# Writing out TensorE's first seven expert items in a two-layer decoder kernel

## The chip, the core and the metric

The kernel runs on one core of one Trainium2 chip. A core has five engines with an instruction stream each: TensorE (PE in the profile), VectorE (DVE), ScalarE (ACT), GpSimd (POOL) and SyncE (SP), and 16 DMA engines that move data between HBM and the on-chip memory (SBUF). TensorE's results go to PSUM, which has eight banks. The engines order their work by semaphores alone. The metric is the device time of one execution in microseconds, the median of several.

## The reference

The input is 256 tokens of width 1024 in float32, the weights are float32 too. Layer 0 is a gated linear recurrence with a dense SwiGLU, layer 1 is a sparse attention followed by a mixture of experts, in which each token goes to two of eight experts. The last part, which the change touches, computes this:

```python
def moe_swiglu(xn, w_router, w_gu, w_down):
    logits = (xn @ w_router).astype(jnp.float32)
    top_v, top_i = lax.top_k(logits, TOP_K)
    top_w = jax.nn.softmax(top_v, axis=-1)
    ...
    for e in range(N_EXPERTS):
        out = out + gates[..., e:e + 1] * swiglu(xn, w_gu[e], w_down[e]).astype(jnp.float32)
```

`w_gu[e]` is 1024 x 7168 (gate and up side by side) and `w_down[e]` is 3584 x 1024: 44.04 MB for one expert, 352 MB for all eight.

## The kernel before, in words

**Stages.** Everything up to the router takes the first 580 us. Then come the *items*. An item is one expert with a tile of up to 96 of the tokens that chose it. Each expert has at least one item; an expert with more than 96 tokens gets another. So there are at least E = 8 items, and the number, which depends on the data, is computed by VectorE and put into SBUF (`route[0:1, ITEMS:ITEMS + 1]`, semaphore `counted`). In the execution shown there are eight.

**One item on TensorE** (lines 2023 to 2033) is 48 *chunks* of weights. A chunk is 128 x 1792 floats, 896 KB by the profile (917,504 bytes). Their order is the table `ITEM`: gate and up of the first half of the hidden columns, gate of the second half, half of the first down part, up of the second half, and the rest. For a gate or up chunk `input_chunk` multiplies the tokens `XT` in three groups of 32 by the chunk, which gives 12 matmuls of 448 columns, each on 32 columns of the array; for a down chunk `down_row` does 12 matmuls of 256 columns for each row of the chunk. Each float32 matmul stands as two in the trace, so that one item has 1440 of them.

**Buffers for the weights.** There are DEEP = 12 slots (six in `ring`, six in `more`). SyncE issues the DMA for chunk m + 12 when TensorE has done with chunk m: `load_item`, lines 672 to 683, waits for `chunk_used` or for a full bank. Chunk m is waited for in `chunk_arrived`, line 543.

**Loops.** All five engines walk over the items in a loop of their own with the item's number in a register. SyncE's covers items 1 to 7 (line 699), with further ones under a condition; ScalarE's is at line 1202 (silu of the gates, copies of the result), VectorE's at line 1579 (product, transposes, and the token tile of the next item with `x_ready`), GpSimd's at line 891 (it loads the rows of a coming item and stores the rows of the one that is done). TensorE's is at line 1986: it waits for `counted`, reads the number of items from SBUF into a register (line 1985), and every wait in the body has a value computed from the loop register, as in

```python
    eng.wait_ge(ready, 16 * (before + m // DEEP + 1) + i * (16 * PER_ITEM // DEEP))
```

Of the kernel before, what the change touches and what calls it, by code (L numbers as in the profile page):

```python
# [58 lines left out]
E, ED = 8, 3584  # L59
# [3 lines left out]
ITEMS = 16  # L63
# [208 lines left out]
def trunk(nc, ins, out):  # L272
# [5 lines left out]
    with ctx:  # L278
# [3 lines left out]
        def sem(name):  # L282
            return ctx.enter_context(nc.semaphore(name))
# [36 lines left out]
        def area(at, *shape, parts=P):  # L320
            n = int(np.prod(shape))
            assert at + n <= AR, (at, n)
            v = arena[0:parts, at:at + n]
            if len(shape) == 1:
                return v
            letters = "abcd"[:len(shape)]
            return v.rearrange(f"p ({' '.join(letters)}) -> p {' '.join(letters)}",
                               **{x: s for x, s in zip(letters[1:], shape[1:])})
# [87 lines left out]
        route = area(11090, 2 * ITEMS).bitcast(I32)  # L416
# [37 lines left out]
        counted, routed = sem("counted"), sem("routed")  # L454
# [80 lines left out]
        def chunk_slot(m):  # L535

            s = m % DEEP
            if s < RING:
                return ring[:, s, 0:WIDE], slot_ready[s], RAW_BASE[s]
            s -= RING  # L540
            return more[:, FIRST_FREE[s // 2] + PAIRS * (s % 2), 0:WIDE], more_ready[s], 0

        def chunk_arrived(eng, m, i):

            v, ready, before = chunk_slot(m)
            eng.wait_ge(ready, 16 * (before + m // DEEP + 1) + i * (16 * PER_ITEM // DEEP))
            return v
# [20 lines left out]
        def bank_count(name, i):  # L568
            b, k = JTURN[name]
            return b, JBASE[b] + k + i * JPER[b]  # L570
# [1042 lines left out]
        def _(pe):  # L1613
            ident, ones, halves = K("ident"), K("ones"), K("halves")

            def mm(o, w, x, start, stop, **kw):
                return pe.matmul(o, w, x, start=start, stop=stop, **kw)  # L1617
# [351 lines left out]
            def gather(n):  # L1969

                b = 6 + n
                for m in range(4):
                    d = 4 * n + m
                    for tt in range(TT):
                        last = mm(ps[:, b, TILE * m:TILE * m + TILE], acc[:, tt, :].rearrange("p (f c) -> p c f", c=KC)[:, d, :], sel[:, tt, :], tt == 0, tt == TT - 1)
                last.then_inc(bank_full[b], 1)
# [4 lines left out]
            for n in range(2):  # L1981
                free_bank(pe, ("gather", n))
                gather(n)
            pe.wait_ge(counted, 1)
            n_items = pe.value_load(route[0:1, ITEMS:ITEMS + 1], min_val=E, max_val=ITEMS - 1)
            with pe.Fori(0, n_items) as i:
                def free(name):
                    b, k = bank_count(name, i)
                    pe.wait_ge(bank_free[b], k)
                    return b  # L1990

                def input_chunk(m, kind, j, c):

                    w = chunk_arrived(pe, m, i)
                    for a in range(GROUPS):
                        b = free((kind, j, a)) if c == 0 else JTURN[(kind, j, a)][0]
                        for n in range(4):
                            last = mm(ps[32 * n:32 * n + 32, b, 0:QUARTER], XT[:, a, c, :], w[:, QUARTER * n:QUARTER * n + QUARTER],
                                      c == 0, c == KC - 1)
                        if c == KC - 1:  # L2000
                            last.then_inc(bank_full[b], 1)
                    if m not in FILLS:
                        last.then_inc(chunk_used, 1)

                def down_row(j, r):

                    first, final = j == 0 and r == 0, j == TILES - 1 and r == ROWS_DN - 1
                    for a in range(GROUPS):
                        b = JTURN[("y", a // 2)][0]
                        if first and a % 2 == 0:  # L2010
                            free(("y", a // 2))
                        at = PIECE * (a % 2)
                        for n in range(4):
                            q, piece = divmod(4 * r + n, PIECES)
                            w = chunk_slot(CHUNK_AT[("dn", j, q)])[0]
                            last = mm(ps[32 * n:32 * n + 32, b, at:at + PIECE], HT[j][:, a, r, :], w[:, PIECE * piece:PIECE * piece + PIECE],
                                      first and a % 2 == 0, final, skip_group_check=True)
                        if final and a:
                            last.then_inc(bank_full[b], 1)
                    if not final and any((4 * r + n) % PIECES == PIECES - 1 for n in range(4)):  # L2020
                        last.then_inc(chunk_used, 1)

                pe.wait_ge(x_ready, i + 1)
                for m, (kind, j, q) in enumerate(ITEM):
                    if kind != "dn":
                        input_chunk(m, kind, j, q)
                        continue
                    if q == 0:
                        pe.wait_ge(hidden_turned, i * TILES + j + 1)
                    chunk_arrived(pe, m, i)  # L2030
                    for r in range(ROWS_DN):
                        if (4 * r + 3) // PIECES == q:
                            down_row(j, r)

# [1 line left out]
_OUT = (1, T, D)  # L2037
# [20 lines left out]
```

## Time and profile before

| | us |
|---|---|
| median of 3 runs | 1516.02 (1512.35 to 1521.06) |
| the profiled execution | 1516.77 |
| its span in the trace | 1515.1 |
| TensorE busy in the span | 1428.1 (94%) |
| VectorE, ScalarE, GpSimd busy | 435.6, 317.1, 149.7 |
| share of TensorE in the chain that ended last | 91%, "issue" 3% |

The span runs from the first to the last instruction that the profiler recorded. "The chain that ended last" is followed back from the last instruction: at each step to what released it, or to the instruction before it on its engine. "Issue" in that chain is time in which the engine waited for nothing that the profile shows. The granted clock is that of TensorE, as a share of 2.4 GHz: 1.0 is the upper level and 0.5 the lower, 1.2 GHz. The DMA share is the mean busy share of the 16 DMA engines; GB/s is what they moved.

### The profile page before, as it was taken

Reading aid. Unit: us, or ns where it says so; the run is one execution under the profiler, and the core shown is the slowest. Engines: PE = TensorE matmul, PEld = TensorE weight load, DVE = VectorE, ACT = ScalarE, POOL = GpSimd, SP = SyncE. Lnnn points to the kernel's source line nnn. Section 1 sums busy time; section 2 is a strip of 40 time slices with the busy share of each in tenths; the row PEclk is TensorE's granted clock in tenths of the full one; section 3 lists DMA queues with packets and bytes.
Section 4 is the critical chain, followed back from the end, with each engine's and each line's share of the span. In section 5 each row is a group of like instructions: output and inputs, shape, how many; then the busy total and the mean of one; then the engine's idle time right before and its main releaser. Section 6 shows DMA issues by size and latency. Waiting matters only on the chain.

```text
span 1515.1 us, 35581 instructions
## 1 busy us (share of the span) xinstructions
PE 1428.1 (94%) x15792; PEld 866.4 (57%) x15792; DVE 435.6 (29%) x645; ACT 317.1 (21%) x507; POOL 149.7 (10%) x219
## 2 busy tenths in 40 slices
PE   8999899999998899998998998998998998998995
PEld 7998799999896584343343343343343343344343
DVE  6864555555557821110110110110110110110111
ACT  5833443443446831000000000000000000000000
POOL 0600010000122715001001001001001001001001
PEclk9999999999998997999999999999999999999998
DMA  9760255555998045999999999999999999999992
GB/s 298 236 200 24 85 168 188 174 178 188 134 294 288 1 164 223 399 418 386 418 410 362 408 407 352 406 406 358 419 408 344 419 410 345 411 410 359 414 418 83
DMA packets 132794, 455.03 MB, mean 300 GB/s; under 512 B 12451, under 2 KB 74108, under 8 KB 132642
## 3 DMA queue, kind: packets, MB, share of 16 engines
q1 hardware_dynamic: 126386, 435.15, 75.2%
q0 software_dynamic: 6080, 17.37, 5.0%
q8 instruction: 136, 2.23, 0.6%
q10 hardware_dynamic: 176, 0.14, 0.0%
q14 instruction: 16, 0.13, 0.0%
HBM read 436.51 MB, written 14.55 MB: 298 GB/s over the span
## 4 chain that ended last, share of the span: by engine, by line
PE 91%; issue 3%; DVE 2%; ACT 2%; DMA 1%; POOL 0%; ACTq 0%; POOLq 0%; DVEq 0%
PE ps L1617 91%; DVE arena L1462 1%; DVE arena L1459 1%; DMA arena<-item_rows,arena 0%; ACT arena L1131 0%; DMA arena<-in_norm_mix_g 0%; ACT x_hi L930 0%; PE ps L1628 0%; PE ps L1865 0%; ACT x_hi L960 0%; DVE arena L1463 0%; ACT between L1152 0%; POOL arena L792 0%; PE ps L1635 0%; ACT arena L1028 0%
## 5 line engine op out<-in xcount | busy, mean ns | idle before, releaser
L1617 PE MATMUL ps<-more,arena 128*32 128x448 f32 x3456 | 328.9, 539 | 0.0
L1617 PE MATMUL ps<-ring,arena 128*32 128x448 f32 x2688 | 275.0, 569 | 31.7 <-issue 30.3
L1586 DVE TENSOR_TENSOR arena<-arena,ps 128x448 f32<-128x448 f32 x48 | 29.8, 621 | 811.0 <-PE ps L1617 807.4
L1617 PEld LDWEIGHTS ps<-more,arena 128*32 128x32 f32 x3456 | 105.8, 110 | 218.9 <-issue 218.9
L1617 PEld LDWEIGHTS ps<-ring,arena 128*32 128x32 f32 x2688 | 85.5, 115 | 213.0 <-issue 211.5
L1617 PE MATMUL ps<-ring,between 128*32 128x256 f32 x3360 | 189.2, 379 | 0.0
L511 DVE TENSOR_TENSOR w_lo<-ring,w_hi 128x2048 fp32r<-128x2048 f32 x67 | 153.3, 2291 | 78.1 <-ACT w_hi L505 78.1
L1617 PEld LDWEIGHTS ps<-ring,between 128*32 128x32 f32 x3360 | 105.5, 110 | 85.8 <-issue 8.1
L505 ACT ACTIVATE w_hi<-ring 128x2048 fp32r<-128x2048 f32 x67 | 127.7, 1911 | 102.8 <-PE ps L1617 96.7
L1617 PE MATMUL ps<-x_hi,w_hi 128*128 128x256 f32 x800 | 113.0, 293 | 9.7 <-ACT x_hi L930 4.4
L1209 ACT ACTIVATE arena<-ps 128x448 f32<-128x448 f32 x48 | 26.1, 544 | 456.5 <-PE ps L1617 456.5
L1617 PE MATMUL ps<-more,between 128*32 128x256 f32 x2016 | 115.3, 379 | 0.0
L1617 PEld LDWEIGHTS ps<-x_hi,w_hi 128*128 128x128 f32 x800 | 103.7, 197 | 15.8 <-issue 10.3
L1617 PE MATMUL ps<-x_lo,w_hi 128*128 128x256 f32 x800 | 105.9, 286 | 0.0
L1617 PE MATMUL ps<-x_hi,w_lo 128*128 128x256 f32 x800 | 104.2, 283 | 0.0
L1617 PEld LDWEIGHTS ps<-x_lo,w_hi 128*128 128x128 f32 x800 | 101.6, 196 | 0.0
L1617 PEld LDWEIGHTS ps<-x_hi,w_lo 128*128 128x128 f32 x800 | 99.6, 192 | 0.1
L881 POOL DMA_DIRECT2D item_rows<-arena x32 | 17.6, 550 | 802.4 <-ACT arena L1216 799.5
L1216 ACT ACTIVATE arena<-ps 128x512 f32<-128x512 f32 (+1 forms) x16 | 7.0, 487 | 427.2 <-PE ps L1617 427.2
L1617 PEld LDWEIGHTS ps<-more,between 128*32 128x32 f32 x2016 | 64.2, 110 | 44.8
L1617 PE MATMUL ps<-hid,w_hi 128*128 128x256 f32 x352 | 63.8, 283 | 0.0
L1617 PE MATMUL ps<-arena 128*128 128x128 f32 (+4 forms) x304 | 51.3, 370 | 7.8 <-DVE arena L1508 2.2
(260 smaller groups left out, 1072.6 us busy)
## 6 DMA issues: line engine op xcount, KB each, us to landing
more<-in_moe_w_gu SPq DMA_DIRECT2D x144, 896.0 KB, 7.8
ring<-in_moe_w_gu SPq DMA_DIRECT2D x112, 896.0 KB, 7.5
ring<-in_moe_w_down SPq DMA_DIRECT2D x80, 896.0 KB, 7.8
more<-in_moe_w_down SPq DMA_DIRECT2D x48, 896.0 KB, 7.8
ring<-in_ffn_w_gu SPq DMA_DIRECT2D x22, 1024.0 KB, 5.1
ring<-in_a_w_in SPq DMA_DIRECT2D x16, 1024.0 KB, 10.6
ring<-in_ffn_w_down SPq DMA_DIRECT2D x11, 1024.0 KB, 5.0
ring<-in_w_kv SPq DMA_DIRECT2D x6, 1024.0 KB, 5.1
```

The costliest lines, as they stand in the source:

```text
L505: eng.activation(w_hi[:, m, :], src, ACT.Copy).then_inc(hi_ready[m], 1)
L511: eng.tensor_tensor(w_lo[:, m, :], ring[:, RAW[name][0], :], w_hi[:, m, :].bitcast(F32), ALU.subtract).then_inc(lo_ready[m], 1)
L881: pool.dma_start(rows_i[:, :, PIECE * n:PIECE * n + PIECE].rearrange("o (a t) d -> t (o a) d", t=32), yt[32 * n:32 * n + 32, :, :]).then_i ...
L1209: act.activation(SU[:, a, :], ps[:, b, 0:QUARTER], ACT.Silu).then_inc(bank_free[b], 1)
L1216: act.activation(yt[:, groups, :], ps[:, b, 0:PIECE * (2 - n)].rearrange("p (a d) -> p a d", d=PIECE), ACT.Copy).then_inc(bank_free[b], 1)
L1459: dve.tensor_tensor(lb, ps[:, k, 0:2 * w].rearrange("p (b t) -> p b t", b=2), BD[:, h:h + 1, T - w:T].to_broadcast([P, 2, w]), ALU.add).th ...
L1462: link(dve.reduce_max(RM[:, s, :], lb, AX.X))
L1586: dve.tensor_tensor(SU[:, a, :], SU[:, a, :], ps[:, b, 0:QUARTER], ALU.mult).then_inc(bank_free[b], 1)
L1617: return pe.matmul(o, w, x, start=start, stop=stop, **kw)
```

## The change

TensorE's loop body becomes a function `item_products(i)`. It is called seven times with a number, i = 0 to 6, and then once inside a loop over the items from 7 on. So the seven calls stand in TensorE's program one behind the other with constant waits, and reading the number of items comes after them. No other engine's program changes, nor does any buffer, transfer or order of matmuls.

```diff
@@ -1981,9 +1981,7 @@
             for n in range(2):
                 free_bank(pe, ("gather", n))
                 gather(n)
-            pe.wait_ge(counted, 1)
-            n_items = pe.value_load(route[0:1, ITEMS:ITEMS + 1], min_val=E, max_val=ITEMS - 1)
-            with pe.Fori(0, n_items) as i:
+            def item_products(i):
                 def free(name):
                     b, k = bank_count(name, i)
                     pe.wait_ge(bank_free[b], k)
@@ -2032,6 +2030,13 @@
                         if (4 * r + 3) // PIECES == q:
                             down_row(j, r)
 
+            for i in range(E - 1):
+                item_products(i)
+            pe.wait_ge(counted, 1)
+            n_items = pe.value_load(route[0:1, ITEMS:ITEMS + 1], min_val=E, max_val=ITEMS - 1)
+            with pe.Fori(E - 1, n_items) as i:
+                item_products(i)
+
```

The end of an item and the start of the next in TensorE's program before: the last chunk's matmuls stand ahead of the branch (line 1986), which goes back to the start of the body. (`more`, `ring` and `between` are weight slots and hidden values in SBUF.)

```order
1408 L1617 MATMUL ps<-more,between 32x256 [waits more_ready5]
1409 L1617 MATMUL ps<-more,between 32x256 x23
1410 L1986 REGISTER_ALU
1411 L1986 COMPARE_AND_BRANCH
1412 L278 UNCONDITIONAL_BRANCH
```

The start of the body, to which the branch returns:

```order
1264 L1985 TENSOR_LOAD arena [waits counted]
1265 L1985 ISA x2
1266 L1986 UNCONDITIONAL_BRANCH
1267 L1986 ISA
1268 L546 ISA [waits x_ready]
1269 L1989 ISA [waits slot_ready0]
1270 L1617 MATMUL ps<-ring,arena 32x448 [waits bank_free0]
1271 L1617 MATMUL ps<-ring,arena 32x448 x3
```

In the changed program the end of item 0 and the start of item 1 stand in a row; such a place comes six times:

```order
1381 L1617 MATMUL ps<-more,between 32x256 [waits more_ready5]
1382 L1617 MATMUL ps<-more,between 32x256 x23
1383 L1617 MATMUL ps<-ring,arena 32x448 [waits bank_free0,slot_ready0,x_ready]
1384 L1617 MATMUL ps<-ring,arena 32x448 x3
1385 L1617 MATMUL ps<-ring,arena 32x448 [waits bank_free1]
1386 L1617 MATMUL ps<-ring,arena 32x448 x3
```

No register instruction and no branch stands between them any more. Between item 6 and item 7 the reading of the number of items and the entry into the loop stand now:

```order
2095 L1617 MATMUL ps<-more,between 32x256 [waits more_ready5]
2096 L1617 MATMUL ps<-more,between 32x256 x23
2097 L2036 TENSOR_LOAD arena [waits counted]
2098 L2036 ISA x2
2099 L2037 UNCONDITIONAL_BRANCH
2100 L2037 ISA
2101 L546 ISA [waits x_ready]
2102 L1987 ISA [waits slot_ready0]
2103 L1617 MATMUL ps<-ring,arena 32x448 [waits bank_free0]
```

These instructions have moved from ahead of item 0 to ahead of item 7. The loop's own branch still stands at the end of the body, behind item 7.

## Rows read from the trace of the kernel before

**Rows 1.** Waits of TensorE from 560 us on: total us, times, longest.
```profile
PE ps L1617 <- issue: 30.3, 7, 5.0
```

**Rows 2.** The chain that ended last, in order: start us, duration us, what.
```profile
580.88 110.89 PE ps L1617 x1440
691.77 5.05 issue
696.82 110.95 PE ps L1617 x1440
...
812.00 111.38 PE ps L1617 x1440
...
927.90 111.46 PE ps L1617 x1440
...
1043.40 110.04 PE ps L1617 x1440
...
1157.45 111.03 PE ps L1617 x1440
...
1273.04 111.26 PE ps L1617 x1440
...
1388.19 109.64 PE ps L1617 x1432
...
1510.80 1.28 DVE arena L1604
```

**Rows 3.** Line 1986, TensorE's loop: count, duration ns min/median/max, first and last start.
```profile
L1986 PEldq COMPARE_BRANCH  x8: 79/5144/5999, 690.4 to 1496.9; - x8
```

**Rows 4.** The same line from 690 to 692 us alone.
```profile
L1986 PEldq COMPARE_BRANCH  x1: 5999/5999/5999, 690.4 to 690.4; - x1
```

**Rows 5.** Stretches behind item 0: length, busy us by engine, granted clock, DMA share, GB/s.
```profile
691.80:694.00 2.20, 0.00 (x0) 0.00 (x0) 0.00 (x0) 0.56 (x2) 0.78 (x2) 1.00 1.04 425
...
696.80:701.00 4.20, 4.18 (x24) 1.20 (x28) 0.00 (x0) 0.00 (x0) 0.00 (x0) 0.50 1.02 413
701.00:702.00 1.00, 1.00 (x12) 0.32 (x8) 0.00 (x0) 0.00 (x0) 0.00 (x0) 0.73 0.89 374
```

**Rows 6.** Line 1985, reading the number of items: duration ns, start us.
```profile
L1985 PEldq TENSOR_LOAD <-arena x1: 487/487/487, 575.0 to 575.0; - x1
L1985 PEldq SEQ_ASSERT  x1: 24/24/24, 575.8 to 575.8; - x1
```

**Rows 7.** Line 1597, VectorE's last step for the next item's tokens: first and last start.
```profile
L1597 DVE TENSOR_TENSOR arena<-arena,x_gain x8: 957/958/960, 669.5 to 1475.9; 128x768 f32<-128x768 f32 x8
```

**Rows 8.** Waits of SyncE from 581 to 1498 us: total us, times, longest.
```profile
SPq L683 <- PE ps L1617: 478.0, 244, 18.9
SPq L680 <- PE ps L1617: 219.0, 128, 2.2
```

**Rows 9.** DMA from 697 to 808 us (item 1): packets and MB, all and by queue.
```profile
DMA packets 7279, 44.86 MB, mean 404 GB/s; under 512 B 893, under 2 KB 893, under 8 KB 7265
...
q0 software_dynamic: 379, 0.77, 2.3%
q8 instruction: 12, 0.20, 0.7%
```

**Rows 10.** DMA from 722 to 760 us.
```profile
DMA packets 2491, 15.91 MB, mean 419 GB/s; under 512 B 275, under 2 KB 275, under 8 KB 2488
```

**Rows 11.** Three stretches of 5 us while rows are stored and loaded (columns of rows 5).
```profile
700.00:705.00 5.00, 5.00 (x52) 1.50 (x44) 0.00 (x0) 0.00 (x0) 1.20 (x3) 0.85 0.95 356
705.00:710.00 5.00, 5.00 (x56) 1.59 (x52) 0.00 (x0) 0.00 (x0) 1.22 (x3) 1.00 1.03 328
710.00:715.00 5.00, 5.00 (x60) 1.64 (x56) 0.00 (x0) 0.00 (x0) 0.00 (x0) 1.00 1.01 330
```

**Rows 12.** Issue to landing of line 683's chunks, 655 to 692 us.
```profile
DMA to landing us min/median/max: 12.9/14.6/15.5
```

**Rows 13.** The same, 1005 to 1039 us.
```profile
DMA to landing us min/median/max: 6.4/7.2/8.0
```

## The prediction

> **What bounds the kernel now.** I read the page first: TensorE is busy for 94% of the span and holds 91% of the chain that ended last, so the question is what stands between its matmuls. TensorE's waits from 560 us on come next [rows 1]: the only large entry is "issue", 30.3 us in seven pieces, the longest 5.0 us. It is a wait for nothing that another engine or a DMA does. The chain in order of time [rows 2] shows where the seven are: one behind each of the first seven items. An item is a solid block of 1440 matmuls, and between the end of item 0 at 691.77 and the start of item 1 at 696.82 there is nothing. From start to start an item takes 115.9 us (696.82 - 580.88).
>
> What the pause is, the rows of TensorE's loop line tell [rows 3]: eight compare-and-branch instructions, with a median of 5144 ns, a longest of 5999 and a shortest of 79. Eight items end with eight branches; seven go back and the last falls through. The first starts at 690.42 and lasts 6.0 us, until 696.42 [rows 4], and the array starts at 696.82. The array ran out at 691.77, so the sequencer had been about 1.35 us ahead of it. The branch is thus the pause: 6.0 - 1.35 + 0.4 = 5.05.
>
> The pause has a second price [rows 5]. The granted clock is 1.00 until 694.00 (2.4 GHz), and it is 0.50 (1.2 GHz) for the 4.2 us after the restart and 0.73 in the next. So some 4.7 us of matmuls run at half rate, which costs 2.4 us more.
>
> The second resource near its limit is the stream of weights. The DMA share is about 1.0 through the items, and an item needs 44.86 MB [rows 9]. But SyncE waits 697 us in total (478.0 + 219.0) for TensorE to free a slot [rows 8], and TensorE never waits for a chunk: today the stream follows TensorE.
>
> **The change, part by part.**
>
> *Seven branches leave the path.* Six boundaries become plain sequence, and at the seventh, between items 6 and 7, the loop is entered rather than repeated. With eight items the loop runs once, and its one branch falls through, as the 79 ns one does. So all seven pauses go, not six: 30.3 us [rows 1].
>
> *Seven cold restarts leave too.* Items 1 to 7 take 110.95, 111.38, 111.46, 110.04, 111.03, 111.26 and 109.64 us [rows 2], together 775.76. Item 1 without its 2.4 us is 108.6; item 0, which also starts cold, stays as it is. I take 108.5 for a warm item, so the seven give back 775.76 - 7 x 108.5 = 16.3 us. Together with the pauses: 46.6 us.
>
> *The entry into the loop before item 7.* Reading the number starts at 575.0 in the old program and its check comes at 575.8 [rows 6]; with the register instructions behind it I count 1.0 us of the sequencer. That fits into its lead of 1.35 us [rows 4], so I take 0. The load did not wait for the array there: at 575.0 the gather products still ran. If the cover is missing, the price is 1 us; the upper end, if entering the loop breaks the stream like a branch does, is one whole pause with its cold restart, 6.7 us ((30.3 + 16.3) / 7). Both `counted` and the number were there 900 us earlier.
>
> *Constants in place of register arithmetic.* The matmuls' pace inside an item is the array's, and it is the same at item ends as in the middle; I take 0, and bound it by 0.3 us an item on either side, half the spread that is left between the items.
>
> *What is late next at a boundary: tokens and banks.* The next item's tokens are ready when VectorE's last step ends, 669.5 + 1.0 us for item 1 [rows 7], 21 us ahead of the end of item 0. Neither `x_ready` nor the gate banks, which ScalarE empties long before, can take the place of the branch: 0 us.
>
> *What is late next: the weights.* This is the term that takes something back. TensorE would use an item's 48 chunks in 108.5 us, 2.26 us each. What the DMA engines can do when there is always work waiting is seen right behind item 0, where the backlog is longest: 419 GB/s from 722 to 760 us [rows 10]. An item is 44.04 MB of weights, 0.79 MB of rows in and out, and 0.20 MB of instructions (the two last as in [rows 9], where the first rows are cut off), 45.0 MB: 107.5 us at 419 GB/s. While the rows move, in small packets, the rate is lower: 356, 328 and 330 GB/s in three stretches of 5 us [rows 11], which loses 5 x (0.15 + 0.22 + 0.21) = 2.9 us. So the stream needs 110.4 us an item, 1.9 more than TensorE.
>
> Against this stands a reserve. A slot comes round every 12 x 2.26 = 27.1 us, and TensorE waits only when issue to landing takes longer than that. At the end of item 0 it is 14.6 us [rows 12], a reserve of 12.5 us. Today every pause lets the stream catch up, and the time to landing is down to 7.2 us by item 3 [rows 13]. Without pauses it grows by 1.9 us an item instead, over seven items by 13.3 us: the reserve is just used up in item 7, and TensorE waits some 0.8 us. The bounds: if an item needs only 109.7 us, no wait at all; if its mean rate is the 404 GB/s that item 1 had over all of its length, 45.0 MB take 111.4 us, the deficit is 2.9 x 7 = 20.5 us and the wait 8 us. Since the reserve is so nearly gone, I take 2 us, nearer to the lower end.
>
> The Trainium skill gives a lower rate for the stream: in "DMA: Bandwidth & Descriptors", section "Bandwidth", some 358 GB/s from HBM for one core where both cores of a domain stream. By that an item would need 123 us and nothing could be gained. The trace disagrees for a core alone, with the 419 GB/s of the row above.
>
> *The sum.* The profiled execution took 1516.8 us, of which 1515.1 are its span. 1516.8 - 30.3 - 16.3 + 2 = 1472.2 us. What lies behind the last item (1497.8 to 1512.1, [rows 2]) moves as it is. The execution is 0.8 us above the median of the runs shown, which spread by 8.7 us: I leave 1472.
>
> **The rivals.**
>
> *The weight stream becomes the bound early.* Every item then takes what the stream needs. For it: a DMA share of 1.0, and a rate of 404 GB/s over item 1. Against it: that stretch holds the rows' slow time already, and 419 was held for 38 us. With 111.4 us an item it is 1472.2 - 2 + 8 = 1478; at 113 us the deficit is 4.5 x 7 = 31.5, less the reserve 12.5, so 19 us of waits: 1489. I name 1483 for the case.
>
> *One pause stays at the entry into the loop:* 1472 + 6.7 = 1479. For it: a branch of the same line number stands there. Against it: in the old program the same four instructions passed without a pause between 575.0 and 580.9.
>
> *Nothing is gained.* This would be so if the stream already needed all of the 115.9 us, the pauses being hidden in it: 1516. Against it speaks that TensorE never waits for a chunk, and that the time to landing falls from 14.6 to 7.2 us.
>
> *Slower: the long program cannot be fetched in time.* An item is 12 packets of the instruction queue, 16 KB each (0.20 MB by 12, [rows 9]), and seven items in a row are 84. Should a part of each fetch be exposed, the array waits at 84 places instead of seven. A branch shows a fetch to last 5 us. The change turns into a loss from 46.6 / 84 = 0.55 us exposed in each; with 1 us it is 1472 + 84 = 1556. Against it: the loop fetches 12 packets in each round now as well, so its body is read in sequence from memory too, and TensorE's blocks show no pause inside.
>
> The Trainium skill says of this in "Runtime: NRT & Kernel Launch", section "Instruction fetch mechanics", that instructions are read ahead in sequence in blocks of 16 KB and that a taken branch whose target is outside the window must wait for a fetch. The trace agrees, with 5.1 us for the branch and packets of that size. In "Advanced Engine Details and Errata", section "Control Flow Timing", a compare-and-branch costs about 108 ns; by that the seven would be worth 0.8 us and the kernel would stay at 1516. Only the branch that falls through, 79 ns, is near it.
>
> **How the numbers follow.** The forecast's case (1467 to 1477) has a chance of 0.68, the early bound by the stream 0.18, a pause left at the entry 0.06, nothing gained 0.04, slower 0.04. What a measurement of this kernel can tell from no change is about 0.5%, 7.6 us. The first three are all faster by over 0.5%: 0.92. No change 0.04, slower 0.04. The range runs from 1466, which allows no wait for chunks and an execution at the lower side of the spread, to 1485, into the middle of the second case; some 0.15 is left outside.
>
> **What would show it.** In the profile after, no "issue" pause of 4 to 5 us between the items, and at most one branch on TensorE's sequencer longer than 0.1 us (none, by the forecast). The items start 108.5 us apart from item 1 on, with a granted clock of 1.0 throughout. The time from issue to landing grows from item to item, from about 15 us to 25 or more in the last, and waits of TensorE for `ring` or `more` come only in items 6 and 7. I am wrong if TensorE waits for chunks from item 2 or 3 on (the stream's rate was mis-sized), if pauses appear inside the items, or if a pause stands before item 7.

## The result, and the profile after

| | us |
|---|---|
| before, median | 1516.24 (1512.35 to 1521.06, 4 runs) |
| changed kernel, median | 1478.36 (1474.24 to 1483.14, 4 runs) |
| ratio | 0.975, 95% interval 0.9709 to 0.9791 |
| profiled execution, span | 1479.12, 1477.5 (before 1516.77, 1515.1) |

The change takes 38 us off. The forecast was 1472, the range 1466 to 1485. The median lies in the range, 1.4 us above the stretch of the forecast's own case (1467 to 1477), and beside the figures of two rivals: 1478 for weights at 404 GB/s and 1479 for a pause left at the loop's entry. The time alone doesn't choose between them; the trace does.

TensorE's loop line in the changed kernel (columns as in [rows 3]):

```profile
L2037 PEldq COMPARE_BRANCH  x1: 98/98/98, 1459.3 to 1459.3; - x1
```

Of the eight branches one is left, the one that falls through. The chain that ended last, in order of time (start us, duration us, what), answers to [rows 2]; pieces under 2 us are left out:

```profile
583.11 576.38 PE ps L1617 x7536
...
1159.65 24.41 DMA ring<-in_moe_w_down
...
1184.10 49.37 PE ps L1617 x768
...
1233.63 25.30 DMA more<-in_moe_w_gu
...
1258.97 88.38 PE ps L1617 x1224
...
1347.53 28.15 DMA more<-in_moe_w_gu
...
1375.72 2.46 PE ps L1617 x24
...
1378.21 7.02 PE ps L1617 x72
...
1385.38 24.66 DMA ring<-in_moe_w_down
...
1410.08 50.23 PE ps L1617 x784
```

There were eight blocks and seven pauses; now one block runs from item 0 well into item 5 (until 1159.5 us), and behind it the chain passes through four chunks of weights. TensorE's waits from 560 us on, beside [rows 1]:

```profile
PE ps L1617 <- DMA more<-in_moe_w_gu: 4.7, 5, 1.1
PE ps L1617 <- DVE arena L1559: 1.3, 1, 1.3
PE ps L1617 <- ACT arena L1198: 1.2, 1, 1.2
PE ps L1617 <- DVE arena L1545: 1.0, 1, 1.0
PE ps L1617 <- DMA ring<-in_moe_w_down: 0.7, 1, 0.7
```

The 30.3 us of "issue" are gone, and 5.4 us of waits for chunks have come. Where these lie, six items show (length, busy us of PE, PEld, DVE, ACT and POOL, granted clock, DMA share, GB/s):

```profile
583.10:693.90 110.80, 110.79 (x1440) 52.49 (x1444) 11.52 (x16) 4.52 (x7) 15.68 (x44) 0.98 0.96 384
694.00:802.20 108.20, 108.20 (x1441) 52.95 (x1436) 11.53 (x16) 4.05 (x8) 4.60 (x9) 1.00 1.02 412
802.40:910.60 108.20, 108.20 (x1441) 52.95 (x1436) 11.53 (x16) 4.07 (x8) 4.60 (x9) 1.00 1.02 411
1127.70:1236.90 109.20, 108.62 (x1440) 48.24 (x1436) 11.45 (x16) 4.03 (x8) 4.60 (x9) 1.00 1.02 412
1237.10:1346.90 109.80, 108.64 (x1440) 46.39 (x1436) 11.34 (x16) 4.06 (x8) 4.61 (x9) 1.00 1.02 410
1347.10:1460.30 113.20, 109.28 (x1440) 46.26 (x1440) 13.76 (x18) 3.84 (x8) 6.62 (x11) 1.00 0.89 359
```

Items 1 and 2 (3 and 4 look the same) are 108.4 us apart at a granted clock of 1.00. Items 5, 6 and 7 are longer by 1.0, 1.6 and 5.0 us. (Item 7 has no start behind it. To the end of its last matmul at 1460.7 us it takes 113.6, and one without a wait takes 108.6, in the run with few rows below. The chain and the window above break off 0.4 us earlier, hence their 113.2.) The time from issue to landing of line 683's chunks in items 1, 2, 3 and 5 tells why, beside [rows 12, 13]:

```profile
DMA to landing us min/median/max: 14.1/15.4/16.3
DMA to landing us min/median/max: 16.0/17.5/18.6
DMA to landing us min/median/max: 19.3/19.7/21.0
DMA to landing us min/median/max: 21.2/23.3/25.3
```

It grows by about 2 us an item, (23.3 - 15.4) / 4, where it had fallen to 7.2. In item 7 the median is 24.1 and the longest 28.0.

### The profile page after: what moved, and what is told of

Read it like the earlier page. It is cut to its first block, busy times and chain, and to the rows that moved or that the text cites. A ratio compares the mean times of both kernels' runs of the same rounds, so it can differ in the third digit from the quotient of the medians.

```text
span 1477.5 us, 35427 instructions
## 1 busy us (share of the span) xinstructions
PE 1415.1 (96%) x15792; PEld 918.9 (62%) x15792; DVE 435.8 (29%) x645; ACT 316.8 (21%) x507; POOL 149.6 (10%) x219
## 3 DMA queue, kind: packets, MB, share of 16 engines
q8 instruction: 124, 2.03, 0.6%
## 4 chain that ended last, share of the span: by engine, by line
PE 86%; DMA 8%; DVE 2%; ACT 2%; issue 1%; POOL 0%; SPq 0%; POOLq 0%; ACTq 0%; DVEq 0%
PE ps L1617 86%; DMA more<-in_moe_w_gu 4%; DMA ring<-in_moe_w_down 3%; DVE arena L1462 1%; DMA ring<-in_a_w_in 1%; DVE arena L1459 1%; DMA arena<-item_rows,arena 0%; PE ps L1865 0%; ACT x_hi L930 0%; ACT arena L1131 0%; ACT x_hi L960 0%; DVE arena L1463 0%; POOL arena L792 0%; ACT arena L1028 0%; ACT arena L1036 0%
## 5 line engine op out<-in xcount | busy, mean ns | idle before, releaser
L1617 PE MATMUL ps<-ring,arena 128*32 128x448 f32 x2688 | 259.7, 543 | 1.2 <-ACT arena L1198 1.2
L1617 PEld LDWEIGHTS ps<-more,arena 128*32 128x32 f32 x3456 | 121.6, 110 | 209.2 <-issue 195.3
L1617 PEld LDWEIGHTS ps<-ring,arena 128*32 128x32 f32 x2688 | 95.3, 111 | 156.1 <-issue 146.7
L1617 PEld LDWEIGHTS ps<-ring,between 128*32 128x32 f32 x3360 | 120.2, 110 | 71.4 <-issue 7.5
L1617 PEld LDWEIGHTS ps<-more,between 128*32 128x32 f32 x2016 | 74.0, 110 | 36.0
L1617 PE MATMUL ps<-arena 128*128 128x128 f32 (+4 forms) x304 | 54.3, 388 | 7.8 <-DVE arena L1508 2.2
```

## The experiments

**Fewer items written out, then six.** The edits are `range(3)` with `Fori(3, n_items)`, and `range(E - 2)` with `Fori(E - 2, n_items)`.

> Items 0 to 2 written out, items 3 to 7 in the loop: four taken branches instead of none. The theory (a taken branch stops the array for 4 to 5 us and the lower clock behind it costs about 2.4 more, 6.7 us together; the weight stream costs the written-out kernel 7.5 us of waits in items 5 to 7, which four pauses would take away) gives 1479 - 7.5 + 4 x 6.7 = 1498 us, with four branches of about 5 us and no wait for chunks. A rival in which the pauses are worth only their idle time (4.3 us) gives 1489 us.

Measured: 1499.61 us (1498.45 to 1501.82), ratio 0.9883 (0.9843 to 0.9923). The price of 6.7 us for a pause with its cold restart holds; with idle time alone it would have been 1489. The *item stage*, from the first matmul of item 0 to the end of item 7's last in the profiled execution, says the same: 897.3 us. Eight items without pause or wait would take 870.0 (110.9 + 6 x 108.42 + 108.6); the changed kernel takes 877.6. TensorE's waits show four pauses and no wait for a chunk; they are a little longer than before (the mean is 4.65 us, before 4.33):

```profile
PE ps L1617 <- issue: 18.6, 4, 5.0
```

> Items 0 to 5 written out, items 6 and 7 in the loop: one taken branch, ahead of item 7. If pause and weight stream add up, 1479 + 6.7 = 1486 us. If the stream uses the pause to catch up, the 5.0 us that item 7 is too long in the written-out kernel go, and the pause costs a net 1.7 us: 1481 us, with item 7 at 110 to 111 us and no wait for chunks in it.

Measured: 1480.17 us (1477.88 to 1480.83), ratio 0.9748 (0.9708 to 0.9787), beside 1481 and 1486. The chain in order of time, from the pause on:

```profile
1345.60 5.25 issue
...
1350.85 109.64 PE ps L1617 x1432
```

Its two branches are the long one, which goes back, and the one that falls through:

```profile
L2037 PEldq COMPARE_BRANCH  x2: 79/3170/6262, 1344.2 to 1459.5; - x2
```

A pause of 5.25 us stands there and the time hardly changes (the item stage is 880.1 us in place of 877.6): item 7 takes 109.6 us where it took 113.2, and waits for no chunk. Pause and weight stream don't add up. Where the stream is nearly late anyway, a pause is spent on it.

**Register values instead of constants.** The seven items stay in a row, in a loop that runs once:

```diff
-            for i in range(E - 1):
-                item_products(i)
             pe.wait_ge(counted, 1)
             n_items = pe.value_load(...)
+            with pe.Fori(E, n_items + 1) as once:
+                for k in range(E - 1):
+                    item_products(once + (k - E))
```

> The seven items are written out in a row as in the changed kernel, but stand in a loop that runs once, so that their waits have register values again; the only thing that returns is the register arithmetic. If the branch is the whole cause, the time is that of the changed kernel, 1478 us within 3, with the first seven items at 108.4 us. If constant waits carry a part of the gain, the items get longer: half of the gain would make it 1497 us.

Measured: 1481.74 us (1476.95 to 1484.02), ratio 0.975 (0.9708 to 0.9792), the changed kernel's ratio. Its items 1 to 4 are 108.4 to 108.5 us apart as well. Constant waits are worth nothing that can be measured; the missing branch is the gain.

**Branches to a near target.**

```diff
             for i in range(E - 1):
                 item_products(i)
+                with pe.Fori(0, 2) as _turn:
+                    pe.wait_ge(counted, 1)
```

> The changed kernel with a small loop of two rounds behind each of the seven written-out items, which holds nothing but a wait that is long fulfilled: seven taken branches again, but with a target a few instructions back. If the price of the old branch is the way to its target (the start of a body of some 3000 instructions, which must be fetched anew), these cost about 0.1 us each, hidden in the sequencer's lead: 1478 us within 3. If a taken branch on TensorE costs 5 us by itself, all pauses are back: 1516 us.

Measured: 1480.02 us (1476.73 to 1482.47), ratio 0.9742 (0.97 to 0.9783). The added line's branches, seven taken and seven not (columns as in [rows 3]):

```profile
L2035 PEldq COMPARE_BRANCH  x14: 76/145/231, 696.7 to 1350.1; - x14
```

The seven taken ones last 0.21 to 0.23 us, the seven not taken 0.08, and together they leave one pause of 0.5 us; a branch back to the start of an item's body takes from 4.7 to 6.3 us. The price is in the way to the target, not in the branch. What the sequencer does in that time, the instruction queue (q8, as in [rows 9]) shows. During the first long branch of the kernel before, 690.4 to 696.4 us, it moves one packet:

```profile
q8 instruction: 1, 0.02, 1.1%
```

It is so in all 19 long branches of the four traces that have them (the kernel before, with 12 slots and with 8, and the two kernels above with fewer items written out): one packet that starts 2.2 to 3.7 us behind the branch's start, and the branch ends 1.4 to 1.5 us behind the packet's end. The branch's length varies by 1.6 us, its distance to that packet by 0.2. So the branch waits for instructions.

**Few rows.** Four lines in `load_rows` and `keep_rows` take one partition in place of 32, so that the items' rows are moved only in part and the kernel's result is incomplete:

```diff
-                    pool.dma_start(item_x[32 * n:32 * n + 32, :, :],
+                    pool.dma_start(item_x[32 * n:32 * n + 1, :, :],
...
-                                   yt[32 * n:32 * n + 32, :, :]).then_inc(rows_kept, 16)
+                                   yt[32 * n:32 * n + 1, :, :]).then_inc(rows_kept, 16)
```

> The changed kernel with the stores and loads of an item's rows cut to one partition in 32 (3 KB in place of 96 KB a transfer), so the items' results are not all kept. If the stream is what makes TensorE wait in items 5 to 7, an item needs some 3.5 us less of it (about 106 us against TensorE's 108.4), the time from issue to landing falls over the items in place of rising by 2 us each, no wait for chunks is left, and the time is 1479 - 7.5 = 1471 us, some 2 less where the stores behind the last item are shorter. If the waits have another cause, 1478 us.

Measured: 1472.81 us (1468.18 to 1473.18), ratio 0.9697 (0.9668 to 0.9725). No wait for a chunk is left: items 1 to 6 are 108.4 to 108.5 us apart and item 7 takes 108.6 to its last matmul's end. The time to landing in items 0, 1, 2, 3 and 5 falls:

```profile
DMA to landing us min/median/max: 9.8/11.7/12.9
DMA to landing us min/median/max: 8.4/9.7/10.7
DMA to landing us min/median/max: 6.6/8.1/9.1
DMA to landing us min/median/max: 6.8/7.2/8.4
DMA to landing us min/median/max: 6.1/7.0/7.3
```

So it is the sum of weights and rows that makes the stream slower than TensorE, not the weights alone.

**The gather of the last item, later.**

```diff
+            pool.wait_ge(more_ready[DEEP - RING - 1], E * (16 * PER_ITEM // DEEP))
             rows_again(0)
             keep_rows(n_before_last)
```

> The changed kernel, but GpSimd waits for the last chunk of the last item to land before it gathers the rows of the first halves (1 MB in two indirect transfers), which now start 15 us into item 7. If these transfers cause the excess of item 7 (5.0 us over a warm item, against 1.0 and 1.6 in items 5 and 6), it shrinks to about 2 us: 1475 us. If it is only the reserve running out, nothing changes: 1478 us. The last step could also come later by what the gather takes, 3 us, if it isn't hidden by the end of item 7: 1478 us too, but with item 7 shorter.

Measured: 1476.72 us (1473.65 to 1478.61), ratio 0.9736 (0.9711 to 0.9762). Item 7 took 110.1 us in place of 113.2, and the chain behind it is no longer: 17.2 us from the end of item 7 in the changed kernel, 17.4 here. The medians differ by less than their spread, so the last experiment takes both again.

**Eight slots, with and without the change.** The edit is `DEEP = 8`.

> The changed kernel with 8 slots for chunks in place of 12. By the corrected reserve, a chunk may take 7 x 2.26 = 15.8 us from issue to landing in place of 11 x 2.26 = 24.9. The time to landing was 13.9 us in item 0, so that TensorE waits from item 0 or 1 on, and the stream sets the pace, 109.3 us an item: 4 x 2.26 = 9 us later than with 12 slots, 1487 us, with waits in every item. If depth doesn't matter and the waits come from bursts alone, 1479 us.

> The kernel before with 8 slots. Each pause lets the stream catch up by 7 us, and from item 2 on the time to landing was 7 us, well under 15.8: only item 0 and 1 may wait for a chunk, 0 to 2 us in all, so 1517 us. If depth alone makes the kernel slower whatever the pauses, it loses the 9 us too: 1525 us.

Measured: 1485.36 us (1484.38 to 1489.48), ratio 0.9794 (0.9765 to 0.9823) for the changed kernel, and 1517.64 us (1512.38 to 1523.64), ratio 1.0002 (0.9982 to 1.0022) for the one before. TensorE's waits for chunks in the first of them:

```profile
PE ps L1617 <- DMA ring<-in_moe_w_gu: 10.6, 11, 1.4
...
PE ps L1617 <- DMA ring<-in_moe_w_down: 1.2, 4, 0.5
```

and in the second only the old pauses, as "issue":

```profile
PE ps L1617 <- issue: 30.7, 7, 5.3
```

With the pauses, four slots less cost nothing; without them 7 us by the medians. The intervals of the two ratios that say so overlap (0.9765 to 0.9823 here, 0.9709 to 0.9791 with 12 slots); the item stages are clearer, 886.9 us against 877.6, 9.3 more, and 4 x 2.26 = 9.0 was expected. Item 2 with eight slots:

```profile
802.30:912.80 110.50, 108.91 (x1444) 46.76 (x1440) 11.41 (x16) 4.15 (x9) 4.60 (x9) 1.00 1.01 410
```

Items 1 to 4 are 110.2 to 110.5 us apart. Here the stream, at a DMA share of 1.01, sets the pace from item 1 on, and so shows its own time for an item: the prediction's 110.4, and not the 109.3 expected ahead of this run. The depth of the buffers is what carries the stream's deficit.

**The changed kernel, the late gather, and a version that goes further,** on one chip. The third also cuts the last item's load of rows, whose values nothing reads:

```diff
-            def load_rows(i, src):
+            def load_rows(i, src, parts=32):
...
-                    pool.dma_start(item_x[32 * n:32 * n + 32, :, :],
+                    pool.dma_start(item_x[32 * n:32 * n + parts, :, :],
...
-            load_rows(n_before_last, item_rows.ap()[bass.ds(n_before_last - 1, 1)])
+            load_rows(n_before_last, item_rows.ap()[bass.ds(n_before_last - 1, 1)], 1)
```

> The changed kernel once more, on the chip and in the rounds of the next two, so that they can be compared. 1478 us within 3. By the theory that the earlier stages' variation accounts for a start of the items between 580 and 587 us, its item stage again takes 877 us (from the first matmul of item 0 to the end of item 7) within 1, wherever it starts.

> The kernel with the late gather once more. If item 7's excess came from the gather, it is again about 3 us shorter in its item stage, 874 to 875 us, and 2 to 3 us faster than the changed kernel on the same chip. If the 1.6 us between the medians was chance, no difference.

> The late gather, and GpSimd's load of rows in the last item, whose values nothing uses, cut to one partition in 32. If the stream's demand in item 7 still makes TensorE wait (item 7 took 110.1 us with the late gather, 1.7 over a warm one), 0.4 MB less of small packets takes about 1 us of it away: 1 us faster than with the late gather. If that rest is the reserve that items 5 and 6 used up, 0 to 0.5 us.

| | median us | ratio to before | items 0 to 7, us |
|---|---|---|---|
| changed kernel | 1479.20 (1474.95 to 1481.99) | 0.9739 (0.9703 to 0.9775) | 877.7 |
| late gather | 1475.55 (1473.59 to 1478.21) | 0.9718 (0.9684 to 0.9752) | 874.8 |
| late gather, short load | 1474.55 (1471.62 to 1476.60) | 0.9710 (0.9675 to 0.9744) | 872.7 |

The last column is the item stage of the profiled execution. Item 7 of the third:

```profile
1347.00:1455.50 108.50, 108.50 (x1447) 48.75 (x1440) 11.89 (x17) 4.09 (x8) 6.53 (x11) 1.00 0.91 368
```

It is as long as an item without any wait. The gather cost about 3 us of item 7 (2.4 in this pair, 3.1 in the earlier one) and the needless load about 2. The intervals of the ratios overlap; that the two steps help rests on the item stages (877.6 and 877.7 against 874.8 twice, and 872.7 once) more than on the medians. For the short load that is a single profile and 1 us between medians whose runs spread by 5. Of the versions that give the whole result the third has the lowest median.

## Why the prediction was right, and where its sizes were off

**The pauses.** Right in kind and size: seven gone, not six, and four put back cost (0.9883 - 0.975) x 1516 + 7.5 = 27.7 us, 6.9 each, where 6.7 had been worked out (the 7.5 are the excess of items 5 to 7 that the pauses take away). Each ratio's interval is worth some 6 us either way; the item stages give 897.3 - 870.0 = 27.3 us, 6.8 each. That the way to the branch's target is the cause had been argued from one line of rows; the short loops and the packets of the instruction queue show it.

**The cold restarts and the warm item.** A warm item is 108.4 us, taken as 108.5. The granted clock is 1.00 over each of items 1 to 7; before, each of them lost some 2.4 us, (775.76 - 7 x 108.42) / 7.

**The entry into the loop.** Taken as nothing, and nothing it is: item 6 ends and item 7 begins at 1347.1 with no pause. (The prediction has the number ready 900 us earlier; from 575 to 1346 us it is 770, which changes nothing.) Reading the number there was as short as in [rows 6]:

```profile
L2036 PEldq TENSOR_LOAD <-arena x1: 487/487/487, 1345.8 to 1345.8; - x1
```

**Register arithmetic.** Nothing, as taken.

**The weight stream.** Its deficit was taken as 1.9 us an item and showed as 2.0, both in the time to landing and in the items with eight slots. The step that was mis-sized is "a slot comes round every 12 x 2.26 = 27.1 us, and TensorE waits only when issue to landing takes longer than that". A slot is free when TensorE has *finished* chunk m, and is needed when it *starts* chunk m + 12: eleven chunks lie between, 24.9 us. The waits in the chain after say it: they end transfers of 24.4, 25.3, 24.7 and 28.2 us (the last is the third of three waits in a row, 3.2 us together). They begin in item 5, where the prediction had them in items 6 and 7 only. The reserve was thus 10.3 us and not 12.5, and seven deficits of 1.9 us leave 3.0 us of waits in place of 0.8.

The second part is a transfer that the sum put at nothing: `rows_again(0)` gathers 1 MB in item 7. Before, where chunks took 10.9 us to land beside it and so had 14 to spare, it was hidden; now it costs about 3 us. "What lies behind the last item moves as it is" looked for it in the wrong place.

The corrected reserve is to be held against the kernel with the late gather: its item stage is 874.8 - 870.0 = 4.8 us too long, where 3.0 come out. The 1.8 us between are open. A deficit of 2.0 in place of 1.9 gives 0.7 of them, and that single chunks land up to 2 us behind the median (25.3 and 23.3 in item 5) may give the rest; no run separates this. The dummy load in item 7, worth about 2 us, is no extra term: the prediction's 45.0 MB for every item hold it.

Items 5 to 7 are 7.5 us too long in all, where 2 had been taken. That is near the 8 us of the prediction's upper bound. The bound had come from a lower rate, which did not show, so that it held the outcome is luck. TensorE's recorded waits for chunks are 5.4 of the 7.5; the rest lies in the same three items without a wait in its name.

**The sum, by its own terms.** The profiled execution took 1479.1 us against 1472.2. Of the 6.9 us, 5.5 are the chunks (7.5 less the 2 in the sum). 0.6 go the other way with the warm item (7 x 0.08). 2.2 lie ahead of item 0, which starts at 583.1 us instead of 580.9; rounding leaves 0.2. What starts item 0 later isn't the change: over the thirteen profiled executions, all with the same earlier stages, it started anywhere from 580.2 to 587.0 us. That it also makes the spread of one kernel's times is likely, but only profiled executions show where the items start.

**The rivals.** That the stream becomes the bound early is false for 12 slots, where items 1 to 4 stand 108.4 us apart without a wait, and true for 8. Nor did its rate of 404 GB/s hold: items 1 and 2 run at 412 and 411. (The 358 GB/s that the prediction's 419 is said to disagree with are, by its own words, for two cores streaming at once. Here one ran, so the row doesn't speak against them.) A pause at the entry, no gain, and a program too long to be fetched did not come: no pause stands inside the written-out items, and the instruction queue moved 2.03 MB in place of 2.23. By the Trainium skill, "Advanced Engine Details and Errata", section "Control Flow Timing", a compare-and-branch is some 108 ns. The near branches are of that size, 76 ns not taken and 214 to 231 taken; the ones that jump back over a whole item aren't. "Runtime: NRT & Kernel Launch", section "Instruction fetch mechanics", separates the two by whether the target is already loaded. The short loops agree, and so does the packet that each long branch waits for.

## What to carry to other kernels

A loop's backward branch costs time when the body is long and the engine is on the critical path. Here it was 4 to 5 us a round on TensorE, some 7 with the slower clock behind it, with 2908 recorded instructions a round. The other four engines have 20 to 194 in theirs, and their branches took 40 to 67 ns, ScalarE's for instance a median of 45. No run shows where between 194 and 2908 the pause sets in.

```profile
L1202 ACTq COMPARE_BRANCH  x8: 40/45/54, 691.9 to 1498.3; - x8
```

Look for "issue" gaps at the same place of each round, and at the branch's own duration.

When such pauses go, ask what used them to catch up. Compare the second resource's time for a round with the engine's, and divide the difference into the reserve, which for n buffers is the time of n - 1 chunks less the time from issue to landing. Then look for transfers that only the slack had hidden.

## What the runs showed that was not expected

A pause in front of an item that would have had to wait for weights is nearly free: the kernel with one long branch ahead of item 7 took 1480.2 us, the one without 1478.4, within the spread; by the item stages it costs 2.5 us in place of 6.8. And four buffers of 0.9 MB each made no difference to the kernel before (ratio 1.0002), while without the pauses they are worth 7 to 9 us. Whether a buffer is needed can't be judged while something else limits the rate.
